# One gather holds two choices of 64 tokens, and one product with two stacked diagonals adds both

## What is computed

```
def peer_ffn(h, lp):                      # 128 tokens at a time
    q = (hx @ wq).reshape(C, PEER_HEADS, 2, PEER_HALF)
    s = einsum('chpd,hpkd->chpk', q, sub_keys)          # 2 x 128 scores
    sv, si = top_k(s, 16)
    comb = sv[:, :, 0, :, None] + sv[:, :, 1, None, :]   # 16 x 16 sums
    fv, fi = top_k(comb, 16)
    idx = e1 * 128 + e2                                  # expert number
    g = softmax(fv)
    u = take(u_tab, idx)
    act = gelu(einsum('chkd,cd->chk', u, hx))
    vv = take(v_tab, idx)
    return einsum('chk,chkd->cd', g * act, vv)
```

## Time and profile before

| | us |
|---|---|
| median of 3 runs | 5726.2 (5720.5 to 5727.7) |
| span of the profiled execution, first to last instruction | 5711.4 |
| busy in the span: TensorE, VectorE, GpSimd, ScalarE | 4961.8, 3898.9, 1548.8, 1433.1 |
| TensorE busy with the product of the experts (L2207) | 2510.4 |
| moved by the queue of the gathers | 1370.7 MB |

### The profile page before, as it was taken

One profiled execution on the slowest core, in us unless ns is written; L12 is line 12 of the kernel. 1 busy time (PEld: TensorE's weight loads), 2 busy tenths in 40 slices (PEclk: granted clock), 3 DMA queues, 4 the chain that ended last, 5 costly groups with the idle time before them and its releaser, 6 DMA issues. The chain is left out here.

```text
span 5711.4 us, 72888 instructions
## 1 busy us (share of the span) xinstructions
PE 4961.8 (87%) x27348; PEld 2704.1 (47%) x27348; DVE 3898.9 (68%) x8899; ACT 1433.1 (25%) x3594; POOL 1548.8 (27%) x1408
## 2 busy tenths in 40 slices
PE   8988899978888888888799888999787988888887
PEld 4545588643343434333245455885433434333332
DVE  4556666548787777777644566665577777777776
ACT  1023211212222232322211232112122222323222
POOL 0100000014444444444300000000144444444443
PEclk9999899989999999999999998999899999999999
DMA  3223610559999999999931245106599999999999
GB/s 142 72 76 133 217 56 32 219 209 427 422 417 426 411 426 416 427 415 426 389 127 69 76 156 194 56 32 229 227 427 426 404 427 410 427 411 427 419 426 390
DMA packets 306822, 1644.50 MB, mean 288 GB/s; under 512 B 34696, under 2 KB 48264, under 8 KB 140832
## 3 DMA queue, kind: packets, MB, share of 16 engines
q0 software_dynamic: 193504, 1370.70, 57.6%
q1 hardware_dynamic: 112960, 269.08, 12.8%
HBM read 1575.84 MB, written 63.82 MB: 287 GB/s over the span
## 5 line engine op out<-in xcount | busy, mean ns | idle before, releaser
L2207 PE MATMUL psum<-peer_rows,peer_diagonal 128*128 128x512 f32 x5120 | 2510.4, 625 | 506.4 <-ACT peer_diagonal L2269 492.0
L2140 POOL DMA_INDIRECT peer_rows<-in_peer_rows,look_up_index x1280 | 1479.9, 1156 | 2890.2 <-PE psum L2207 1632.6
L2350 DVE CUSTOM_DVE_ANT_0 peer_rows<-peer_rows,h_rows 128x1024 f32<-128x1024 f32 x1280 | 1552.9, 1226 | 480.8 <-DMA peer_rows<-in_peer_rows,look_up_index 468.3
L2207 PEld LDWEIGHTS psum<-peer_rows,peer_diagonal 128*128 128x128 f32 x5120 | 936.1, 198 | 1537.1 <-issue 848.6
L2263 ACT ACTIVATE peer_active<-peer_dots 128x2 f32<-128x2 f32 (+1 forms) x642 | 130.7, 204 | 2020.6 <-DVE peer_dots L2350 2020.4
L2269 ACT ACTIVATE peer_diagonal<-ident_sb,peer_weight 128x128 f32<-128x128 f32 x1280 | 444.4, 394 | 145.0 <-DVE peer_weight L2303 143.2
L2154 PEld LDWEIGHTS psum<-h_sb,query_weights 128*128 128x128 f32 x1184 | 236.4, 200 | 306.2 <-issue 306.2
L471 PE MATMUL psum<-in_weights,h_sb 128*128 128x512 f32 (+1 forms) x800 | 309.9, 549 | 0.0
L2303 DVE TENSOR_TENSOR peer_weight<-peer_active,peer_share 128x2 f32<-128x2 f32 (+1 forms) x642 | 103.7, 162 | 200.5 <-ACT peer_active L2263 200.2
L1006 PE MATMUL psum<-h_sb,rw_in_gate_weights 128*128 128x512 f32 (+1 forms) x768 | 214.0, 440 | 28.9 <-DMA rw_in_gate_weights<-in_w_gate 28.9
L2154 PE MATMUL psum<-h_sb,query_weights 128*128 128x128 f32 x1184 | 236.0, 282 | 0.0
(11 more groups left out here) (378 smaller groups left out, 5880.2 us busy)
## 6 DMA issues: line engine op xcount, KB each, us to landing
rw_out_mod_weights<-in_w_mod SPq DMA_DIRECT2D x16, 2048.0 KB
in_weights<-in_w_in SPq DMA_DIRECT2D x12, 2048.0 KB, 8.7
peer_rows<-in_peer_rows,look_up_index POOLq DMA_INDIRECT x1280
scratch_rw_scratch<-rw_in_direction SPq DMA_DIRECT2D x20, 768.0 KB, 6.4
wkv_own<-scratch_rw_scratch SPq DMA_DIRECT2D x20, 768.0 KB, 5.3
rw_in_gate_weights<-in_w_gate POOLq DMA_DIRECT2D x24, 512.0 KB, 6.3
scratch_rw_scratch<-rw_in_z SPq DMA_DIRECT2D x10, 1024.0 KB, 5.4
wkv_r_kk<-scratch_rw_scratch SPq DMA_DIRECT2D x40, 256.0 KB, 6.2
```

The costliest lines, as they stand in the source:

```text
L2140: nc.gpsimd.indirect_dma_start(rows[spot][:, :], None, t.dram["peer_rows"], bass.IndirectOffsetOnAxis(ap=index[j % 4][:, k:k + 1], axis=0) ...
L2207: last = nc.tensor.matmul(t.bank[2 * (i % 2) + c], diagonal[k % DIAGONALS][:, :], rows[spot][:, D + c * 512:D + (c + 1) * 512], start=(j = ...
L2350: v.tensor_tensor_reduce(rows[spot][:, 0:D], rows[spot][:, 0:D], h[:, :], 1.0, 0.0, ALU.mult, ALU.add, dots[b][:, k:k + 1]).then_inc(s["do ...
```

## The change

A gather now takes two choices of 64 tokens instead of one choice of 128. Gather k of a unit serves the tokens of half k % 2 (0 to 63 for even k, 64 to 127 for odd k); its partitions 0 to 63 hold the rows of choice k // 2 and its partitions 64 to 127 those of choice k // 2 + 8 of the same 64 tokens. The number of gathers, their 128 rows and their bytes stay.

What follows from it:

- `number_experts` writes the indices with four VectorE instructions of 64 partitions x 8 columns instead of one of 128 x 16, and `share` is written by four instead of one.
- `h_rows` is kept twice, `[128, 2, 1024]`: for each half of the tokens, their h stands on both halves of the partitions. `copy_h_rows` writes it with eight ScalarE copies of 64 x 512 instead of two of 128 x 512, in the context stage and at each end of a tile. VectorE waits for them by choice: four before the dot of k = 0, all eight before that of k = 1.
- The diagonal is 128 x 64: two 64 x 64 diagonals one above the other, made from a new constant `pair_ident`, which is loaded at the start of the program.
- The product of a gather has 64 columns of weights and writes 64 partitions of the bank, the lower half for even k and the upper for odd k. TensorE now waits once for the diagonals of a pair and then runs the four products of the pair in the order first 512 columns of k and k + 1, second 512 columns of k and k + 1. What it does ahead for other units (`project_next`, `next_query` and so on) for both choices of the pair stands before that wait.
- At the very end the two halves of the result wait for three and four signals, instead of one and two.
- `chosen` shares its memory with `sums_rest`.

```diff
@@number_experts@@
-        v.tensor_tensor(self.index[buffer][:, :], number[:, :], expert[:, 1, :], ALU.add).then_inc(looked_up, 1)
+        for g, tokens in enumerate(HALVES):
+            for a, rows in enumerate(HALVES):
+                last = v.tensor_tensor(self.index[buffer][rows, :].rearrange("p (k g) -> p g k", g=2)[:, g, :], number[tokens, PARTS[a]],
+                                       expert[tokens, 1, PARTS[a]], ALU.add)
+        last.then_inc(looked_up, 1)
+
+ROW_COPIES = 8
+
+def copy_h_rows(nc, t, banks, copied):
+    for g, tokens in enumerate(HALVES):
+        for rows in HALVES:
+            for half in range(2):
+                nc.scalar.copy(t.h_rows[rows, g, half * 512:(half + 1) * 512], banks[half][tokens, :]).then_inc(copied, 1)
@@peer_stage, TensorE@@
-                        pe.wait_ge(s["diagonal"], n * TOPK + k + 1)
-                        spot = place_of(n * TOPK + k)
+                        pe.wait_ge(s["diagonal"], n * TOPK + hi)
                         for c in range(2):
-                            last = nc.tensor.matmul(t.bank[2 * (i % 2) + c], diagonal[k % DIAGONALS][:, :], rows[spot][:, D + c * 512:D + (c + 1) * 512],
-                                                    start=(j == 0 and k == 0), stop=(j == HEADS - 1 and k == TOPK - 1))
-                            if i == TILES - 1 and j == HEADS - 1 and k == TOPK - 1:
-                                last.then_inc(s["summed"], 1)
-                        if not (i == TILES - 1 and j == HEADS - 1 and k == TOPK - 1):
-                            last.then_inc(s["mixed"], 1)
+                            for k in range(lo, hi):
+                                last_of_tile = j == HEADS - 1 and k >= TOPK - 2
+                                done = nc.tensor.matmul(t.bank[2 * (i % 2) + c][HALVES[k % 2], :], diagonal[k % DIAGONALS][:, :],
+                                                        rows[place_of(n * TOPK + k)][:, D + c * 512:D + (c + 1) * 512],
+                                                        start=(j == 0 and k < 2), stop=last_of_tile)
+                                if i == TILES - 1 and last_of_tile:
+                                    done.then_inc(s["summed"], 1)
+                                elif c == 1:
+                                    done.then_inc(s["mixed"], 1)
@@peer_stage, ScalarE@@
             def copy_rows(i):
-                for half in range(2):
-                    act.wait_ge(s["turned"], 2 * (i - 1) + half + 1)
-                    nc.scalar.copy(h[:, half * 512:(half + 1) * 512], next_banks[half]).then_inc(s["row_copied"], 1)
+                act.wait_ge(s["turned"], 2 * i)
+                copy_h_rows(nc, t, next_banks, s["row_copied"])
...
-                            nc.scalar.activation(diagonal[k % DIAGONALS][:, :], t.ident[:, :], ACT.Identity, scale=weight[b][:, k:k + 1]).then_inc(s["diagonal"], 1)
+                            nc.scalar.activation(diagonal[k % DIAGONALS][:, :], t.pair_ident[:, :], ACT.Identity, scale=weight[b][:, k:k + 1]).then_inc(s["diagonal"], 1)
@@peer_stage, VectorE@@
-                if i:
-                    dve.wait_ge(s["row_copied"], 2 * i)
...
-                    weights.step(v.tensor_scalar(share[b][:, :], power[b][:, :], inverse[b][:, 0:1], None, ALU.mult))
+                    for g, tokens in enumerate(HALVES):
+                        for a, places in enumerate(HALVES):
+                            weights.mark(v.tensor_scalar(share[b][places, :].rearrange("p (k g) -> p g k", g=2)[:, g, :], power[b][tokens, PARTS[a]],
+                                                         inverse[b][tokens, 0:1], None, ALU.mult))
+                    weights.wait_all()
...
+                            if i and j == 0 and k < 2:
+                                dve.wait_ge(s["row_copied"], ROW_COPIES * i - (ROW_COPIES // 2 if k == 0 else 0))
                             dve.wait_ge(landed[spot], ((n * TOPK + k) // RING + 1) * 16)
-                            v.tensor_tensor_reduce(rows[spot][:, 0:D], rows[spot][:, 0:D], h[:, :], 1.0, 0.0, ALU.mult, ALU.add,
+                            v.tensor_tensor_reduce(rows[spot][:, 0:D], rows[spot][:, 0:D], h[:, k % 2, :], 1.0, 0.0, ALU.mult, ALU.add,
...
-                dve.wait_ge(s["summed"], c + 1)
+                dve.wait_ge(s["summed"], c + 3)
```

51 lines of the change are left out of this document (28 added, 23 removed).

## The result

The changed kernel takes 5751.3 us (median of 7 runs, 5744.9 to 5767.0) where the kernel before took 5727.7 on the same chip (7 runs, 5720.5 to 5737.6): a ratio of 1.0044, with a 95% interval from 1.0028 to 1.0060. It is slower by about 24 us (16 to 34). One of the 29 executions of the kernel before that ran beside shares_early and its group took 15114 us, and it is left out of every ratio. The forecast was 5735, within 0.2%; the time lies above that bound, inside the range, and next to the rival on the slow side (5750).

What follows compares the result with a forecast made beforehand. Gathers at 427 GB/s were taken to bound the kernel. Tile ends +5.2, other unit ends +1, context stage +0.8 and layer ends +2 gave +9 us on 5726.2: 5735 us, range 5715 to 5754.

Steps and rivals of the forecast that it cites:

- What bounds the kernel: Expert stages: gathers at 427 GB/s set a floor the change keeps; only 41 us of loss against it could be won.
- The hole: The 7 us after each tile's end, when transfers run dry: 2.3 us lost each, 18.6 in all, before the change.
- 2.8 - 0.5 + 0.3 - 0.3: Per tile end, us: six more copies, last pair's products, waits and diagonals, second buffer of the new tile's first pair.
- my premise that every microsecond on this chain widens the hole by one: Tile's end, gelu to first new gather: each added microsecond costs one, since the ring has run dry behind it.
- My 0 for the first pair of the new tile: Its two buffers come back together, as late as the first one came before: 0 us.
- The catch-up: The 70 us after the hole: 17.7 us lost before; less TensorE work was to gain 1.65 us an end.
- The other ends of units: 60 unit ends inside tiles: the ring has room, six small VectorE instructions cost some 0.5 us; 0 to +8, likeliest +1 us.
- The clock falls everywhere: Rival: TensorE runs at the lower clock in steady pairs and at 60 unit ends too; 5750 us, +24, chance 0.25.
- The products do not overlap: Rival: every pair stays at 3.7 us and nothing is caught up; +32 us, 5758 us, chance 0.05.
- Copies hidden: Rival: the copies at tile ends cost nothing and the catch-up goes; -16 to -20 us, 5708 us, chance 0.07.
- The clock holds: Rival: TensorE stays at 2.4 GHz through the ends, so last pairs save 1.8 us; -5, 5721 us, chance 0.15.
- The end of the program: End of each layer, last pair shorter but single choices slower at the lower clock: +1 us a layer, together +2.

Runs made afterwards that it cites:

- shares_early: Changed kernel with the next unit's inverse and shares computed behind the seventh pair of a unit; ratio to the kernel before 1.0058.
- before_pair_order: Kernel before with only TensorE's new order: one wait for both diagonals of a pair, products still 128 wide; ratio 1.0054.
- behind_shares_early: Changed kernel with h_rows copied behind the last pair's diagonals and shares computed behind a unit's seventh pair; ratio to the kernel before 0.9997.
- warm_clock: Changed kernel with four products by zeros ahead of each pair's wait for its diagonals, except a unit's last pair; ratio to the kernel before 1.0057.
- twice_warm: turned_twice with shares mostly behind the fourth pair and four zero products ahead of each pair's work from a tile's third unit; ratio to the kernel before 1.0000.
- before_eight_copies: Kernel before with eight ScalarE copies of 64 x 512 at each tile's end instead of two of 128 x 512; 5763.3 us against 5727.8.
- turned_twice: behind_shares_early with the next tile's h turned for both halves, so four copies of 128 x 512 replace eight; ratio to the kernel before 0.9988.
- before_small_pieces: Kernel before with indices and shares each written by four VectorE instructions of 64 x 8 instead of one; 5741.1 us against 5727.8.

## Why the prediction was right or wrong

- **What bounds the kernel** was right. TensorE lost 627 us of work and nothing was won; the loss sits against 427 GB/s, which the rest of the tile still moves in shares_early.
- **The hole** was right nearly to its number. I had 2.8 - 0.5 + 0.3 - 0.3 = 2.3 us for each end, 18.4 in all; the 20 us stretches lose 41.2 - 22.4 = 18.8 more. Single terms moved: the copies cost 3.3 us (0.54 each instead of 0.47), and the last pair's products at the lower clock 3.68 against 3.70, so -0.5 should have been 0. With both, the chain grew by 3.66 us an end on average, as measured from the last gelu to the first gather, and not by about 2.6. That only 18.8 / 8 = 2.35 us of transfers were lost in these stretches speaks against my premise that every microsecond on this chain widens the hole by one; the agreement of the sum is in part luck. My 0 for the first pair of the new tile holds: the first gather comes 4.82 us after the gelu (5116.46 - 5111.64), before 4.94. before_pair_order shows that this is a balance: with wide products it comes after 6.68.
- **The catch-up** failed in its sum: I had -13 us, the profile shows +2.6 (14.3 to 16.9). One reason is a price I had put at nothing, that of TensorE's order: with wide products it takes this stretch to 29.2, and against that the narrow ones win 12.3, about what I had hoped for. The other is the pieces, which alone take it to 24.3. How these add in one kernel is inferred. With the shares out of the way the loss here fell to 6.6 in shares_early and 7.7 in behind_shares_early; but the early shares alone make it 8.5 in the kernel before, so that at most 2 us of this are a gain of the narrow products.
- **The other ends of units** failed by as much: +1 forecast, 15.6 more loss in the rest of the tile. I took 0.5 us for the pieces, nearly all of it hidden by the ring's room. The chain grew by some 1.55 us, 1.67 at the end shown: I took six more instructions as 0.5 us back to back, and the four shares alone take 1.0 to 1.3 us where one took 0.23. And it is not all hidden: in the kernel before 0.97 us of it cost 13 us. The rest of the tile went from a loss of 1.0 to 16.6, and back to 1.0 in the profile of shares_early at a clock of 0.864, though the medians of that run show no gain.
- **The rival "The clock falls everywhere"** came nearest in time (5750) and was right on the clock, which fell to 0.866 on average. Its price is not borne out. The Trainium skill, in TensorE: Matmul & The Clock Gate, HAM oscillation, describes a kernel whose engine waits for transfers between bursts and loses throughput because every burst starts at the half clock. TensorE's pairs pay here too, 3.48 to 3.68 us for a pair instead of 1.94, but no run shows a gain in the program's time from holding the clock up. In warm_clock the rest of the tile lost 9.1 instead of 16.6, so the clock may add to what the pieces do; with the shares moved away (twice_warm) the ratio stayed at 1.0000. In both, the work that holds the clock up has a cost of its own, so its worth is not isolated.
- **The rival "The products do not overlap"** fell: 1.94 us a pair at the full clock. **"Copies hidden"** fell: they had been on the chain, at the price of before_eight_copies. **"The clock holds"** fell.
- **The signs I named.** The hole widened, the last pair's products start 5.08 us after the gelu (I said 4.4), and pairs take 1.94 us. The 70 us after an end did not reach 427 GB/s (418 in the stretch shown), and the rest of the tile moves 419 to 426 where it moved 426 to 427: steady stretches lost their full rate in part, which I had named as a sign of being wrong.
- **The end of the program**: I had +1 us a layer. From the last dot to the last instruction on x it took 5702.50 - 5696.17 = 6.33 us and takes 5748.13 - 5742.18 = 5.95, 0.4 less (the two rows below, of the changed kernel). This term had the wrong sign in the second layer, at a size that does not matter.

```profile
5742.18 1.23 DVE L2373 CUSTOM_DVE_ANT_0 peer_rows<-peer_rows,h_rows 128x1024 f32<-128x1024 f32 x1 [0.78 <-DMA peer_rows<-in_peer_rows,look_up_index]
...
5747.44 0.69 DVE L2394 TENSOR_TENSOR x_sb<-x_sb,peer_out 128x512 f32<-128x512 f32 x1
```

The parts do not add. Alone in the kernel before they cost 35, 31 and 13 us, 79 together; the change costs 24. Copies and order widen the same hole and slow wide products, which the narrow ones do not suffer as much. That the narrow products give back the difference is inferred from this sum: no run had them alone. No run put the four index instructions back into one in the changed kernel either, so their share is not separated from that of the shares. What also stays open is why the refill after a tile's end takes longer in turned_twice than in behind_shares_early, and how much of the change's 24 us is the pieces (13 by before_small_pieces, 9 by behind_shares_early, nothing by the medians of shares_early).

## What to carry to other kernels

When a reshaped product halves an engine's work, price first what it makes the other engines do to feed it, at the points where they stand in a row: here 862 us less of product time gave less than six more copies at a tile's end, six more small instructions at a unit's end and a later release of the first buffer of a pair cost. Small instructions between two batches want a price of their own: one on a quarter of the data took nine tenths of the time, and here one microsecond more in that chain cost 13 us although half a microsecond less gained nothing that could be measured. Put such work where its engine waits for transfers, and copies behind the work that others wait for; both together brought the kernel back to the time of before (0.9997).
